# Running sums in the seven-product blocks of a fused three-model kernel, and 16 more blocks in that form

## The chip, the cores and the metric

One core of one Trainium2 chip. The metric is the device time of one execution in microseconds, as the median of three runs: 1971.0 us for the kernel before (1969.97 to 1972.1).

## The reference, cut to what matters

x (1, 256, 1024) in float32 goes through three models one after the other: a first one with two layers (latent attention, then a gated recurrence), here called A and B; a second one of two hybrid layers, L0 and L1; a third one of one layer, C. The change touches L0, L1 and C alone. What is computed of a hybrid layer, around the change:

```python
h = rms_norm(x, norm1_g)
q, k, v, iq, ik, iw, a_in, c_in, g_in = jnp.split(h @ w_in, IN_SPLITS, axis=-1)
y_attn = dsa_attention(q, k, v, iq, ik, iw) @ w_attn_out      # indexer scores, top 64 keys, softmax
a_val, a_gate = jnp.split(a_in, 2, axis=-1)
a = causal_dwconv(a_val * sigmoid(a_gate), conf_conv_w) + conf_conv_b      # 31 taps
y_conf = silu(layer_norm(a)) @ w_conf_out
c_b, c_c, c_x = jnp.split(c_in, 3, axis=-1)
y_sc = (c_b * causal_dwconv(c_c * c_x, sc_conv_w)) @ w_sc_out              # 3 taps
merged = g0 * y_conf + g1 * y_attn + g2 * y_sc                             # g = sigmoid(g_in)
x = x + merged @ w_o
u = causal_dwconv(rms_norm(x, norm2_g) @ w_up, ffn_conv_w) + ffn_conv_b
x = x + (silu(u_gate) * u_val) @ w_down
```

All products are float32. C has retention, block-sparse attention, a gated merge and a feed-forward part of the same sizes.

## The kernel before

Features lie on the partitions, the 256 tokens on the free axis. The weights come in blocks of 128 x 2048 float32 (1 MB) into a ring of two slots, `ring`, by SyncE's queue (L675), in a fixed order (`stream_plan`). SyncE waits for `slot_done` of the slot and, after a seven-product block, for its event `mixed`. Each engine has one queue, written out by hand in its own function, and semaphores between them. One block gives 256 output features for 256 tokens from 1024 input features.

There are two kinds of blocks. A plain one (`halves`) is 16 matmuls of 128x128 weights with 256 columns. A seven-product one (`fast_block`, or `late_block`, where the input comes late) is a Strassen-Winograd form: the block is seen as 2x2 quarters, and seven products of 4 matmuls with 128 columns are made, 28 in all, in place of eight quarter products. A float32 matmul is two instructions in the trace. Its inputs are:
- sums of the input's quarters, made once for a stage by VectorE (`token_sums`, `sum_acts`, L2275 to L2280);
- differences of the weight's quarters, made by GpSimd for each block (`mix`, L1793 to L1805): "mix1" and "mix1b" as one instruction of 1024 columns (L1798), then "mix2" (L1802) and "mixed" (L1805) of 512. For the first block of a stage mix1 and mix1b are two instructions (L1793, L1795). GpSimd waits until the block has landed and the block before in the same buffer is done. It has no other queue for them.

TensorE computes the seven products in the order w0, w3, w2 (slot released here, with `slot_done`), m0, m1, m2, m3, where w are the quarters as they come and m the mixed ones. Each product has its own 128 columns in one of two PSUM banks, "x" and "y". Four main banks make two pairs, taken in turn, so that a block needs the pair of the block two before it. ScalarE copies the first product to `p1c` (`first_product`, L1474). VectorE makes the four output quarters with five adds (`unite`, L2256 to L2265) and frees both banks. VectorE's queue is in the order in which the results are wanted, so an operation in front of a `unite` delays the bank's release.

The stretch that the change rewrites lies in each of L0 and L1 between the gate blocks `g` (12 seven-product blocks) and the attention heads. TensorE's order there: `cx0` (4 seven-product blocks: half of c_c and c_x), among them the small products `spread` and `index_products`; `cx1` (4 plain blocks: the other half); the sums for the layer norm; `cb` (4 plain blocks: c_b); then eight heads, each with one block of `conf` or `sc`. VectorE meanwhile ends the 31-tap convolution (`convolved`, 248 steps of 256 columns with the sum in PSUM), rotates iq, q and k (`rotate_in_place`), adds up the indexer's `scores`, centres the convolution's result (`centred`), does the 3-tap convolution (`short_conv(0)`, `short_conv(1)`: 4 products, 4 first taps, 8 more taps each), finds the top 64 keys (`ranked`, max and match_replace), and makes the mask. ScalarE does the Relu of the indexer (`index_terms`), copies the plain blocks `cx1` out of PSUM, squares for the norm, and issues small transfers from its queue (L1596).

## Time and profile before

| | |
|---|---|
| Median of three runs | 1971.0 us |
| The profiled execution, span from first to last instruction | 1967.1 us |
| The same execution's own time, span and what lies around it | 1971.0 us |
| TensorE busy | 1954.6 us, 99% of the span |
| VectorE busy | 1194.6 us, 61% |
| GpSimd busy | 1119.2 us, 57% |
| ScalarE busy | 402.2 us, 20% |
| Blocks in L0, L1, C that become chained blocks | 195, of them 16 plain before |

Rows of the timeline read: start in us, duration in us, engine, line of the kernel, operation, output tile, input tiles, how many instructions are merged in the row, and in brackets how long the engine was idle before and what ended that. Consecutive instructions of one kind are merged, and a row that begins where another one still runs belongs to a pipelined engine. L712 is the one place from which all matmuls are issued, so a block is told by its operands: `ring` for quarters as they came, `arena` or `h_res` for mixed ones.

### The profile page before, as it was taken

To read this page: it belongs to the slowest core of one execution; us is meant where nothing else is said; L and a number is where in the kernel's file an instruction comes from. 1 tells how busy PE (TensorE), PEld (TensorE's weight loads), DVE (VectorE), ACT (ScalarE), POOL (GpSimd) and SP (SyncE) were. 2 spreads that over 40 slices of the span, in tenths; PEclk is the share of its full clock that TensorE was granted. 3 is DMA by queue.
4 is the path that set the end of the run, shared out by engine and by line. 5 is a ranking of instruction groups with operands and counts; after the bars stand their busy time and mean duration, and the time that the engine had idled before them with its cause. 6 is when DMAs were issued, how large, how long until landed. Compare 5 with 4: busy or idle time off the path is not lost. (4 is left out here: it accounts for less than half of the span.)

```text
span 1967.1 us, 37363 instructions
## 1 busy us (share of the span) xinstructions
PE 1954.6 (99%) x14834; PEld 1848.6 (94%) x14834; DVE 1194.6 (61%) x3033; ACT 402.2 (20%) x978; POOL 1119.2 (57%) x750
## 2 busy tenths in 40 slices
PE   9999999999999999999999999999999999999999
PEld 7788889999899999999999899999999999999998
DVE  4244535989978477524888987667713487554541
ACT  2241521111321222110111222222102025220000
POOL 1000038785176588758678155487776674448783
PEclk9999999999999999999999999999999999999999
DMA  5313445444444454445444343454444442445544
GB/s 212 134 43 132 150 151 179 160 164 139 149 144 143 156 174 167 171 148 172 168 159 168 121 162 131 150 172 172 167 164 161 136 147 97 140 150 172 172 161 140
DMA packets 44267, 299.76 MB, mean 152 GB/s; under 512 B 5440, under 2 KB 6592, under 8 KB 10176
## 3 DMA queue, kind: packets, MB, share of 16 engines
q1 hardware_dynamic: 42560, 295.42, 43.7%
q8 instruction: 119, 1.95, 0.4%
q10 hardware_dynamic: 1536, 1.97, 0.3%
q14 instruction: 52, 0.43, 0.1%
HBM read 294.35 MB, written 1.05 MB: 150 GB/s over the span
## 5 line engine op out<-in xcount | busy, mean ns | idle before, releaser
L712 PE MATMUL bank<-arena,ring 128*128 128x128 f32 (+2 forms) x3854 | 603.4, 310 | 1.2 <-ACT arena L1344 0.6
L712 PEld LDWEIGHTS bank<-arena,ring 128*128 128x128 f32 x3854 | 540.4, 191 | 43.6 <-ACT arena L1344 3.1
L712 PE MATMUL bank<-xn,ring 128*128 128x128 f32 (+3 forms) x3104 | 467.8, 306 | 0.0
L712 PEld LDWEIGHTS bank<-xn,ring 128*128 128x128 f32 (+1 forms) x3104 | 424.4, 191 | 31.1 <-issue 4.4
L712 PE MATMUL bank<-arena 128*128 128x128 f32 (+3 forms) x3048 | 391.5, 284 | 0.0
L712 PEld LDWEIGHTS bank<-arena 128*128 128x128 f32 (+1 forms) x3048 | 364.9, 192 | 9.3 <-issue 1.5
L712 PE MATMUL bank<-arena,h_res 128*128 128x128 f32 x2696 | 322.4, 276 | 2.1 <-POOL h_res L1802 1.2
L712 PEld LDWEIGHTS bank<-arena,h_res 128*128 128x128 f32 x2696 | 310.6, 192 | 5.1 <-POOL h_res L1802 2.4
L1798 POOL TENSOR_TENSOR arena<-ring 128x1024 f32<-128x1024 f32 (+1 forms) x103 | 243.0, 2360 | 124.7 <-DMA ring<-wstream 124.2
L1798 POOL TENSOR_TENSOR h_res<-ring 128x1024 f32<-128x1024 f32 (+1 forms) x95 | 221.7, 2334 | 127.1 <-DMA ring<-wstream 111.9
L1849 DVE SCALAR_TENSOR_TENSOR bank<-arena,par,bank 128x256 f32<-128x256 f32 x640 | 259.5, 483 | 15.3 <-DVE arena L2265 7.7
L1474 ACT ACTIVATE p1c<-bank 128x128 f32<-128x128 f32 x192 | 52.3, 272 | 730.8 <-PE bank L712 730.5
L2259 DVE TENSOR_TENSOR partial<-bank,p1c 128x128 f32<-128x128 f32 x192 | 55.0, 286 | 225.1 <-PE bank L712 224.8
L1805 POOL TENSOR_TENSOR h_res<-ring,h_res 128x512 f32<-128x512 f32 (+1 forms) x111 | 144.3, 1300 | 8.7
L1802 POOL TENSOR_TENSOR h_res<-h_res,ring 128x512 f32<-128x512 f32 (+1 forms) x111 | 143.8, 1296 | 8.7
L1766 POOL TENSOR_TENSOR sq<-sq 128x256 f32<-128x256 f32 (+1 forms) x45 | 34.7, 772 | 187.7 <-ACT sq L1347 169.3
L1793 POOL TENSOR_TENSOR h_res<-ring 128x512 f32<-128x512 f32 x16 | 20.4, 1276 | 211.8 <-DVE arena L2280 83.6
L1802 POOL TENSOR_TENSOR arena<-arena,ring 128x512 f32<-128x512 f32 (+1 forms) x103 | 133.4, 1295 | 8.1
L1805 POOL TENSOR_TENSOR arena<-ring,arena 128x512 f32<-128x512 f32 (+1 forms) x103 | 132.9, 1291 | 8.1
L2256 DVE TENSOR_TENSOR bank<-bank,p1c 128x128 f32<-128x128 f32 x80 | 23.6, 296 | 147.1 <-ACT p1c L1474 145.4
L1313 ACT ACTIVATE arena<-bank 128x256 f32<-128x256 f32 (+6 forms) x104 | 44.0, 424 | 206.1 <-PE bank L712 140.6
L712 PE MATMUL bank<-xn,h_res 128*128 128x128 f32 x648 | 84.9, 276 | 1.1 <-POOL h_res L1805 1.1
(241 smaller groups left out, 1805.0 us busy)
## 6 DMA issues: line engine op xcount, KB each, us to landing
ring<-wstream SPq DMA_DIRECT2D x264, 1024.0 KB, 4.8
ring<-wstream SPq DMA_DIRECT2D x16, 768.0 KB, 4.2
cst<-consts SPq DMA_DIRECT2D x1, 2488.0 KB, 14.7
h_res<-tokens SPq DMA_DIRECT2D x2, 544.0 KB, 5.1
arena<-arena ACTq DMA_DIRECT2D x16, 64.0 KB, 3.4
out<-arena SPq DMA_DIRECT2D x4, 256.0 KB, 5.4
arena<-arena ACTq DMA_DIRECT2D x28, 32.0 KB, 3.1
ring<-wstream SPq DMA_DIRECT2D x2, 288.0 KB, 2.9
```

Of the source, the lines that this page charges most:

```text
L712: return pe.matmul(o, lhs, rhs, start=start, stop=stop, skip_group_check=True)
L1313: ins = act.activation(dst, psum[b][0:rows, 0:T], func, **kw)
L1474: act.activation(p1c[:, b // 2 % 2, :], psum[b][:, 0:P], ACT.Copy).then_inc(*e.step((key, "p1")))
L1766: pool.tensor_tensor(out=acc, in0=acc, in1=squares[:, j, 0:T], op=ALU.add).then_inc(*e.step(event))
L1793: pool.tensor_tensor(out=m[:, 0:size], in0=w[:, size:2 * size], in1=w[:, 0:size], op=ALU.subtract).then_inc(*e.step(("mix1", block)))
L1798: pool.tensor_tensor(out=m[:, 0:2 * size], in0=w[:, size:3 * size], in1=w[:, 0:2 * size], op=ALU.subtract).then_inc(*e.step(("mix1", block)))
L1802: pool.tensor_tensor(out=m[:, 2 * size:3 * size], in0=m[:, size:2 * size], in1=w[:, 0:size], op=ALU.add).then_inc(*e.step(("mix2", block)))
L1805: pool.tensor_tensor(out=m[:, 3 * size:4 * size], in0=w[:, 3 * size:4 * size], in1=m[:, 2 * size:3 * size], op=ALU.subtract).then_inc(*e.s ...
L1849: return dve.scalar_tensor_tensor(out=out, in0=a, scalar=scalar, in1=b, op0=op0, op1=op1)
L2256: dve.tensor_tensor(view[:, 0, 0, :], x[:, 2 * P:3 * P], p1, ALU.add).then_inc(*e.step((key, "c11")))
L2259: dve.tensor_tensor(u2, y[:, 3 * P:4 * P], p1, ALU.add).then_inc(*e.step((key, "u2")))
```

## The change

The seven products of a block (all but those of `down` and the first of `attn`) are now added up in PSUM as running sums, in two banks of 256 used columns. The quarters c11, c12 and c21, c22 lie beside each other. ScalarE copies the running sums out four times per block (`snapshot` 1, 5, 2, 3) into `snaps`, two buffers in turn; TensorE waits for the first three before it goes on adding to the same columns. `unite` is one VectorE add of 512 columns. The slot is released after the sixth product, not after the third. SyncE waits for "spent", the last mix that reads the slot. A stage's first block is mixed in the order mix1, mix2, mixed, mix1b. The plain blocks `cx1` and `cb` become chained blocks too: `cx` has eight, `cb` four, and GpSimd mixes for them. ScalarE's other work is put between the snapshots. VectorE's order in the stretch changes: the convolution takes 12 steps per block (10 before) and ends after the last gate block, centring comes after the second unite of `cx`, the first ranking is split 3, 2, 3. GpSimd's partial sums for the layer norm come two gate blocks earlier, and the gathering of its squares two blocks later.

```diff
+            def chain_block(block, plain, sums, ready=None, token_major=False):
+
+                slot = e.next_block()
+                w = ring[:, slot, :].rearrange("p (s k c) -> p s k c", s=4, c=P)
+                m = mixed_of(block).rearrange("p (s k c) -> p s k c", s=4, c=P)
+
+                def product(place, weight, act, opens=False):
+                    half, col = part_at[place]
+                    for k in range(4):
+                        one, two = (act(k), weight[:, k, :]) if token_major else (weight[:, k, :], act(k))
+                        ins = mm(bank[half], slice(0, P), slice(col, col + P), one, two, opens and k == 0, k == 3)
+                    return ins
+
+                pe.wait_ge(*e.landed(slot))
+                bank, emptied = e.take_pair(block)
+                for when in emptied:
+                    pe.wait_ge(*when)
+                for event in ready or ():
+                    pe.wait_ge(*e.at(event))
+                product("c22", w[:, 0], lambda k: plain(0, k, 0), opens=True).then_inc(*e.done("main_done", ("pe", (block, "p1"))))
+                product("c11", w[:, 3], lambda k: plain(1, k, 0), opens=True)
+                pe.wait_ge(*e.at((sums, "sum", 0)))
+                pe.wait_ge(*e.at(("mix1", block)))
+                product("c12", m[:, 0], lambda k: sums_at_k(sums, 0, k)).then_inc(*e.done("main_done", ("pe", (block, "p5"))))
+                pe.wait_ge(*e.at((block, "s1")))
+                pe.wait_ge(*e.at((sums, "sum", 1)))
+                pe.wait_ge(*e.at(("mix2", block)))
+                product("c22", m[:, 2], lambda k: sums_at_k(sums, 1, k))
+                pe.wait_ge(*e.at(("mixed", block)))
+                product("c21", m[:, 3], lambda k: plain(1, k, 1)).then_inc(*e.done("main_done", ("pe", (block, "p4"))))
+                pe.wait_ge(*e.at((block, "s5")))
+                pe.wait_ge(*e.at((sums, "sum", 3)))
+                product("c12", w[:, 2], lambda k: sums_at_k(sums, 3, k)).then_inc(*e.done(f"slot_done{slot}"))
+                pe.wait_ge(*e.at((block, "s2")))
+                pe.wait_ge(*e.at((sums, "sum", 2)))
+                pe.wait_ge(*e.at(("mix1b", block)))
+                product("c22", m[:, 1], lambda k: sums_at_k(sums, 2, k)).then_inc(*e.done("main_done", ("pe", (block, "t"))))
...
+                def cx(n):
+
+                    chain_block((F, "cx", n // 2, n % 2), of_tokens(xn), (F, "x"))
+
+                cx(0)
                 spread()
-                cx0(F, 1)
-                cx0(F, 2)
+                cx(1)
+                centre_sums(L + "ln", 1, lambda j: sel[:, 0, :], [(L + "ln", "total")])
+                cx(2)
                 pe.wait_ge(*e.at((L + "ikr",)))
                 pe.wait_ge(*e.at((L + "iqr",)))
                 index_products(0, 3)
-                cx0(F, 3)
+                cx(3)
                 index_products(3, 6)
-                halves(L + "cx1", 0, 8, [P, P], x256, S)
+                cx(4)
                 index_products(6, 8)
-                halves(L + "cx1", 1, 8, [P, P], x256, S)
-                centre_sums(L + "ln", 1, lambda j: sel[:, 0, :], [(L + "ln", "total")])
-                halves(L + "cx1", 2, 8, [P, P], x256, S)
-                halves(L + "cx1", 3, 8, [P, P], x256, S)
+                cx(5)
                 b = e.take("beside", (L + "ln", "var"))
                 pe.wait_ge(*e.emptied((L + "ln", "var")))
                 for n, (event, j) in enumerate((((L + "ln", "acc"), 0), ((L + "ln", "sq", 6), 6), ((L + "ln", "sq", 7), 7))):
                     pe.wait_ge(*e.at(event))
                     ins = mm(b, slice(0, P), slice(0, S), C("ones"), sq[:, j, 0:S], n == 0, n == 2)
                 ins.then_inc(*e.side_done((L + "ln", "var")))
+                cx(6)
+                cx(7)
...
+            def snapshot(key, n):
+
+                done, of, to = {1: ("p1", "c22", "c11"), 5: ("p5", "c12", "c22"), 2: ("p4", "c22", "c12"), 3: ("t", "c22", "c21")}[n]
+                (half, col), at = part_at[of], snap_at[to]
+                if n == 1 and snap_before(key):
+                    act.wait_ge(*e.at((snap_before(key), "c22")))
+                act.wait_ge(*e.at(("pe", (key, done))))
+                act.activation(snap(key)[:, at:at + P], psum[e.bank_of((key, half))][:, col:col + P],
+                               ACT.Copy).then_inc(*e.step((key, f"s{n}")))
+
+            def snapshots(key, *meanwhile, early=None):
+
+                snapshot(key, 1)
+                snapshot(key, 5)
+                if early:
+                    early()
+                snapshot(key, 2)
+                for work in meanwhile:
+                    work()
+                snapshot(key, 3)
...
+                snapshots((F, "cx", 0, 0), lambda: gate_tanh_l(11), queries_rms)
+                snapshots((F, "cx", 0, 1))
                 act.wait_ge(*e.at((L + "qkn", 0)))
                 for a, b in ((0, 16), (16, 0)):
                     act.dma_start(qk[a:a + 16, 8:10, :], qk0[b:b + 16, 8:10, :]).then_inc(k_halves, 16)
-                first_product((F, "cx0", 1, 0))
-                index_terms(0, 3)
-                first_product((F, "cx0", 1, 1))
-                index_terms(3, 6)
-                product_in(1, 0)
-                index_terms(6, 8)
-                product_in(1, 1)
-                centred_squares(L + "ln", 8, lambda j: ac[:, j, :])
-                product_in(1, 2)
-                product_in(1, 3)
-                root((L + "ln", "var"), sq[:, 0, 0:S], D, RMS_EPS, (L + "ln", "rms"))
-                act.wait_ge(*e.at((L + "rotated", "q")))
-                for it in range(4):
-                    act.dma_start(qk0[0:32, 2 * it:2 * it + 2, :], qk[32 * it:32 * it + 32, 0:2, :]).then_inc(q_back, 16)
-                for j in range(8):
-                    bias = G(f"{LN_B}.{l}", j)
-                    act.wait_ge(*e.at((L + "zn", j)))
-                    act.activation(yc[:, j, :], ac[:, j, :], ACT.Identity, bias=bias).then_inc(*e.step((L + "z", j)))
-                    act.activation(ac[:, j, :], ac[:, j, :], ACT.Tanh, bias=bias).then_inc(*e.step((L + "zt", j)))
+                snapshots((F, "cx", 1, 0))
+                index_terms(0, 2)
+                snapshots((F, "cx", 1, 1), early=lambda: index_terms(2, 3))
+                index_terms(3, 5)
+                snapshots((F, "cx", 2, 0), rotary_back, lambda: centred_squares(L + "ln", 8, lambda j: ac[:, j, :]), early=lambda: index_terms(5, 6))
+                snapshots((F, "cx", 2, 1), early=lambda: index_terms(6, 8))
+                snapshots((F, "cx", 3, 0), ln_root)
+                snapshots((F, "cx", 3, 1), lambda: norm_gates(0, 2))
+                for q, (first, last) in enumerate(((2, 4), (4, 6), (6, 8), (8, 8))):
+                    snapshots((F, "cb", q, 0), lambda: norm_gates(first, last))
...
+                if block[2:] == (0, 0) and block[1] in ("a", "g", "conf", "o", "up", "mqk", "ret"):
+                    t1, t3, t2, t4 = (m[:, size * c:size * c + size] for c in range(4))
+                    w11, w12, w22, w21 = (w[:, size * c:size * c + size] for c in range(4))
+                    pool.tensor_tensor(out=t1, in0=w12, in1=w11, op=ALU.subtract).then_inc(*e.step(("mix1", block)))
+                    pool.wait_ge(*e.at(("mix1", block)))
+                    pool.tensor_tensor(out=t2, in0=w22, in1=t1, op=ALU.subtract).then_inc(*e.step(("mix2", block)))
+                    pool.wait_ge(*e.at(("mix2", block)))
+                    pool.tensor_tensor(out=t4, in0=w21, in1=t2, op=ALU.subtract).then_inc(*e.step(("mixed", block)))
+                    pool.tensor_tensor(out=t3, in0=w22, in1=w12, op=ALU.subtract).then_inc(*e.step(("mix1b", block)))
+                    e.counts.events["spent", block] = e.counts.events["mix1b", block]
+                    return
...
+            def unite(key, out, cols, *after):
+
                 for event in after:
                     dve.wait_ge(*e.at(event))
+                if len(key) == 4 and chained(key):
+                    dve.wait_ge(*e.at((key, "s3")))
+                    by = "p t (n c) -> p n t c" if key[1] in ("v", "mv", "rv") else "p n (t c) -> p n t c"
+                    x = e.bank_of((key, "x"))
+                    both = banks[:, 512 * x:512 * x + 1024].rearrange("p (t z) -> p t z", t=2)[:, :, 0:2 * P]
+                    dve.tensor_tensor(out[:, :, cols:cols + S].rearrange(by, c=P), both.rearrange("p t (n c) -> p n t c", c=P),
+                                      snap(key).rearrange("p (n t c) -> p n t c", n=2, t=2),
+                                      ALU.add).then_inc(*e.frees((key, "x"), (key, "c11")))
+                    e.counts.events[key, "c12"] = e.counts.events[key, "c22"] = e.counts.events[key, "c11"]
+                    dve.wait_ge(*e.at((key, "c11")))
+                    return
...
-                    convolved(10 * it, 10 * it + 10)
+                    convolved(12 * it, 12 * it + 12)
...
                     unite((F, "g", it, 0), sg[:, 2 * it:2 * it + 2, :], 0)
-                    if it < 11:
-                        convolved(90 + 10 * it, 100 + 10 * it)
-                convolved(200, 214)
-                cx0_in(0)
+                    convolved(108 + 35 * it // 3, 108 + 35 * (it + 1) // 3)
...
+                cx_in(0)
                 spread_norm(L + "qk", range(1), G(g("k_norm_g_2"), 0), qk0[:, 8:10, :], qk0[:, 8:10, :], L + "qkn")
                 query_scales(L + "qk", P ** -0.5)
                 dve.wait_ge(iq_halves, 64 * (l + 1))
                 rotate_in_place(iq0[:, :, :], iq[:, :, :], "idx", slice(0, P), (L + "iqr",))
-                cx0_in(1)
-                convolved(214, 224)
-                cx0_in(2)
-                dve.wait_ge(*e.at((L + "iws",)))
-                scores(0, 3)
-                convolved(224, 232)
-                cx0_in(3)
-                scores(3, 6)
-                convolved(232, 8 * CK)
-                scores(6, 8)
+                cx_in(1)
                 if l == 0:
                     for j in range(ND):
                         dve.wait_ge(*e.at(("N3", "xn", j)))
                 centred(L + "ln", 8, lambda j: ac[:, j, :])
+                cx_in(2)
+                dve.wait_ge(*e.at((L + "iws",)))
+                scores(0, 3)
+                cx_in(3)
+                scores(3, 6)
                 dve.wait_ge(q_rows, 192 * (l + 1))
                 rotate_in_place(qk[:, 0:2, :], qk[:, 2:4, :], "attn", slice(0, P), (L + "rotated", "q"))
+                cx_in(4)
+                scores(6, 8)
                 dve.wait_ge(k_halves, 32 * (l + 1))
                 rotate_in_place(qk0[0:32, 8:10, :], qk[0:32, 8:10, :], "attn", slice(0, 32), (L + "rotated", "k"))
...
+                    pair = slice(2 * q, 2 * q + 2)
+                    unite((F, "cb", q, 0), both_p, 0, *([(L + "ys", 2 * q - 1)] if q else [(L + "ac", 6), (L + "ac", 7)]))
                     for t in range(2):
-                        j, key = 2 * q + t, (L + "cb", q, t)
-                        dve.wait_ge(*e.at(("pe", key)))
-                        dve.wait_ge(*e.at((L + "sct", j, 2)))
-                        dve.tensor_tensor(ys[:, j, :], psum[e.bank_of(key)][:, 0:S], ys[:, j, :],
-                                          ALU.mult).then_inc(*e.frees(key, (L + "ys", j)))
+                        dve.wait_ge(*e.at((L + "sct", 2 * q + t, 2)))
+                    dve.tensor_tensor(ys[:, pair, :], both_p, ys[:, pair, :], ALU.mult).then_inc(*e.step((L + "ys", 2 * q + 1)))
...
                 short_conv(0)
-                ranked(0, TOPK // 16)
+                cx_in(5)
+                ranked(0, 3)
                 dve.wait_ge(*e.at((L + "ln", "rms")))
                 dve.reciprocal(sq[:, 0, 0:S], sq[:, 0, 0:S]).then_inc(*e.step((L + "ln", "inv")))
                 dve.wait_ge(*e.at((L + "ln", "inv")))
+                cx_in(6)
                 for j in range(ND):
                     stt(ac[:, j, :], ac[:, j, :], G(g(LN_G), j), sq[:, 0, 0:S], ALU.mult, ALU.mult).then_inc(*e.step((L + "zn", j)))
+                cx_in(7)
+                short_conv(1)
                 branch_b(0)
-                short_conv(1)
+                ranked(3, 5)
                 branch_b(1)
                 for j in range(ND):
                     dve.wait_ge(*e.at((L + "zt", j)))
@@ -2482,7 +2615,7 @@
                 for j in range(ND):
                     dve.wait_ge(*e.at((L + "yc", j)))
                 token_sums((F, "yc"), yc)
-                ranked(TOPK // 16, TOPK // 8)
+                ranked(5, TOPK // 8)
                 branch_b(2)
```

## Rows read from the trace of the kernel before

**Rows 1.** The page: busy time of each engine, and granted clock in 40 slices.
```profile
PE 1954.6 (99%) x14834; PEld 1848.6 (94%) x14834; DVE 1194.6 (61%) x3033; ACT 402.2 (20%) x978; POOL 1119.2 (57%) x750
...
PEclk9999999999999999999999999999999999999999
```
**Rows 2.** TensorE's waits, the largest: line, releaser, total us, times, longest us.
```profile
PE bank L711 <- DVE arena L2146: 2.1, 3, 0.8
```
**Rows 3.** Timeline of TensorE in C.up: w2 ends where these rows start.
```profile
1799.73 2.84 PE L712 MATMUL bank<-arena 128*128 128x128 f32 x24
...
1805.99 2.84 PE L712 MATMUL bank<-arena,h_res 128*128 128x128 f32 x24
```
**Rows 4.** Timeline of TensorE in L0: stretch's start, plain cb, first head.
```profile
455.88 1.95 PE L712 MATMUL bank<-xn,ring 128*128 128x128 f32 x16
...
516.74 27.79 PE L712 MATMUL bank<-xn,ring 128*128 128x256 f32 x128
544.37 0.82 PE L712 MATMUL bank<-arena 128*128 128x128 f32 x4
...
552.13 0.55 PE L711 MATMUL bank<-cst,arena 128*128 128x128 f32 x3 [0.69 <-DVE arena L2146]
```
**Rows 5.** Timeline in C.up: one block's adds on VectorE, ScalarE's copy.
```profile
1803.83 0.42 DVE L2261 TENSOR_TENSOR partial<-bank,partial 128x256 f32<-128x256 f32 x1
...
1805.12 0.69 DVE L2753 TENSOR_TENSOR arena<-arena,bank 128x512 f32<-128x512 f32 x1 [0.20 <-DVE bank L2265]
...
1806.19 0.28 ACT L1474 ACTIVATE p1c<-bank 128x128 f32<-128x128 f32 x1 [5.98 <-PE bank L712]
```
**Rows 6.** Timeline of GpSimd in L0.up and C.up; the first row is TensorE's.
```profile
703.73 2.84 PE L712 MATMUL bank<-arena,h_res 128*128 128x128 f32 x24
...
710.21 2.36 POOL L1798 TENSOR_TENSOR h_res<-ring 128x1024 f32<-128x1024 f32 x1 [2.52 <-DMA ring<-wstream]
...
1798.45 2.36 POOL L1798 TENSOR_TENSOR h_res<-ring 128x1024 f32<-128x1024 f32 x1 [1.10 <-DMA ring<-wstream]
...
1802.23 1.26 POOL L1805 TENSOR_TENSOR h_res<-ring,h_res 128x512 f32<-128x512 f32 x1
1804.93 2.35 POOL L1798 TENSOR_TENSOR arena<-ring 128x1024 f32<-128x1024 f32 x1 [1.44 <-DMA ring<-wstream]
...
1807.36 1.60 POOL L1802 TENSOR_TENSOR arena<-arena,ring 128x512 f32<-128x512 f32 x1
```
**Rows 7.** Timeline of L0's stretch: GpSimd, VectorE alone, ScalarE's transfers.
```profile
475.60 1.27 POOL L1805 TENSOR_TENSOR arena<-ring,arena 128x512 f32<-128x512 f32 x1
...
514.13 3.24 DVE L1849 SCALAR_TENSOR_TENSOR arena<-arena,par 128x256 f32<-128x256 f32 x8
...
516.95 2.44 ACTq L1596 DMA_DIRECT2D arena<-arena  x4
...
542.55 1.27 POOL L1793 TENSOR_TENSOR h_res<-ring 128x512 f32<-128x512 f32 x1 [34.06 <-issue]
```
**Rows 8.** Busy time in windows of L0's stretch: PE, PEld, DVE, ACT, POOL.
```profile
455.90:500.00 44.10, 44.10 (x321) 40.88 (x320) 40.34 (x95) 8.15 (x18) 17.93 (x12) 1.00 0.37 127
...
516.70:544.40 27.70, 27.70 (x130) 24.37 (x130) 27.46 (x92) 8.37 (x18) 1.85 (x2) 1.00 0.48 162
```
**Rows 9.** VectorE's adds in SBUF while GpSimd works: L0's heads, attn, C.up.
```profile
608.34 2.35 POOL L1798 TENSOR_TENSOR arena<-ring 128x1024 f32<-128x1024 f32 x1 [2.83 <-DMA ring<-wstream]
609.46 1.37 DVE L2275 TENSOR_TENSOR arena<-arena 128x128 f32<-128x128 f32 x1 [1.57 <-ACT arena L1313]
...
610.87 1.31 DVE L2277 TENSOR_TENSOR arena<-arena 128x128 f32<-128x128 f32 x1
...
627.54 1.37 DVE L2275 TENSOR_TENSOR arena<-arena 128x256 f32<-128x256 f32 x1
...
1805.85 1.98 DVE L2275 TENSOR_TENSOR arena<-arena 128x512 f32<-128x512 f32 x1
```
**Rows 10.** Timeline of TensorE: the first matmuls of the program.
```profile
1.11 6.05 PE L712 MATMUL bank<-sq 128*128 128x256 f32 x16 [1.11 <-POOL small L1750]
```

284 lines of the change are left out of this document (155 added, 129 removed).

## Prediction

> **What bounds the kernel now.** I read the page first: TensorE is busy for 1954.6 of the 1967.1 us of the profiled span, VectorE for 1194.6, GpSimd for 1119.2 [rows 1]. The list of TensorE's waits, read next, adds up to some 9 us in 11 pairs; the largest is 2.1 us in three waits of up to 0.8 us [rows 2]. So the time is the sum of TensorE's blocks. A change gains only if it shortens that sum, and loses whatever it makes TensorE wait. The timeline of C.up gives the price of a seven-product block: the third product ends at 1799.73 in one block and at 1805.99 in the next, so 6.26 us for 56 recorded instructions [rows 3]. The four plain blocks L0.cb run from 516.74 to 544.37, 6.91 us each [rows 4].
>
> **The gain.** 16 plain blocks become seven-product blocks: 16 x (6.91 - 6.26) = 10.4 us off TensorE. The other blocks keep their 28 products, so nothing is gained there on TensorE. VectorE's five adds per block (of 0.28 to 0.42 us, 1.7 us in all) become one add of 512 elements, like the 0.69 us ones beside them [rows 5]. That is about 1.0 us less VectorE work per block, off the path. ScalarE copies four times instead of once, 0.28 us each, starting 0.2 us behind TensorE [rows 5]. A snapshot that TensorE waits for is thus there 0.2 + 0.28 + about 0.1 = 0.6 us after its product. TensorE does 8 of its 28 matmuls (1.8 us) in between for the first two snapshots and 4 of them (0.9 us) for the third. It is free as long as ScalarE does nothing else at that moment.
>
> **The slack that the new order uses up.** The ring slot is released after 12 of 28 matmuls before, after 24 of 28 now: 12/28 x 6.26 = 2.7 us later. GpSimd starts the next subtraction 5.20 us behind the release (release 1799.73, start 1804.93) and has all three done 5.04 us after its start (1798.45 to 1803.49) [rows 3, 6]. So the last mix is there 5.4 + 5.2 + 5.0 - 12.5 = 3.1 us after the start of the block that needs it; it was needed at 5.4 us, and is now needed at 3.6 us. A slack of 4.9 us becomes 0.4 to 0.5 us, in all 195 changed blocks. What eats it: (a) late landings. GpSimd starts at 710.21 for a slot released at 703.73, 6.5 us [rows 6]; seven such blocks (5.99 to 7.65 us) lie in stages without other cover, and what they have over the slack adds to 5 us. (b) VectorE's sums over SBUF in the up stages lengthen a mix from 1.27 to 1.60 us [rows 6]; two groups of four per up stage, 0.5 us each, three stages: 3 us. (c) The second block of six stages, whose mix starts late because the first one's is on the path: 0.5 us each, 3 us. Sum 11 us; bounds 3 (most of it covered) and 20 (each twice as often).
>
> **The stretch that decides.** GpSimd does nothing for the plain blocks: it ends its mixes at 476.87 and starts the next at 542.55, after 34 us in which it had nothing to do [rows 7]. In that gap VectorE is fully busy: 40.34 of 44.10 us in its first part, 27.46 of 27.70 us in its last [rows 8]. Rows from L0's head stage show what happens when both are busy: VectorE's 128x128 add takes 0.28 us alone, and 1.37, 1.31, 1.31 us while GpSimd subtracts; each one ends 0.1 us after a GpSimd instruction ends, one per GpSimd instruction [rows 9]. I see this for all operations with two SBUF inputs and for tensor_scalar between SBUF tiles, and for none that reads PSUM (the 0.69 us ones of rows 5 ran under a subtraction), nor for max, match_replace and reciprocal. By the Trainium skill (SBUF — State Buffer, "Who interferes with whom") a VectorE instruction with two SBUF inputs contends with a GpSimd one that reads SBUF, and the pair is locked for a whole instruction; by that rule, which speaks against this change, the trace agrees.
>
> The new blocks bring 3 subtractions each, 5.0 us, so GpSimd works 5.0 of every 6.3 us through the stretch. VectorE's operations there that need the shared reads are some 90 a layer: rotations of iq, q, k (9), 8 to centre, 16 scores, two short convolutions of 16 (3.24 us for eight of one's, alone [rows 7], 5.6 us with the cheaper eight), 8 + 8 of the norm and its gate, 4 sums, 4 of the mask: about 38 us alone. The others (12 unites, ranking, products from PSUM, the end of the convolution) are about 33 us.
>
> Walked through L0, with time 0 at the end of the last gate block (455.88) [rows 4]; landings by 5.1 us, one such operation per mix while GpSimd has work, free running when it has none:
> - cx block 3 starts at 13.8. The three rotations of iq alternate with its mixes: last mix at 18.8, needed at 17.6, and the one before just late. TensorE waits 1.6 us.
> - cx block 4 starts at 22.9. Its third snapshot stands on ScalarE behind a Relu that waits for the first score, which stands on VectorE behind eight centring subtractions (four of them alternate with mixes) and a unite: score at 30.1, snapshot 30.8, needed 28.3. Waits 2.6 us.
> - cx block 6 starts at 41.8. Its first snapshot stands behind rotary_back (VectorE's rotation done at 42.6, then four DMA issues, 2.44 us for four [rows 7]), eight squares (2.8 us) and the fourth snapshot of block 5: done at 48.5, needed at 44.5. Waits 4.0 us.
> - cx block 8 wants its pair of banks at 59.8. VectorE's unite that frees it stands behind four scores, three rotations and the first short convolution: 23 operations, ten of them held by a mix, done at 72.0. Waits 12.3 us.
> - cb block 3 wants its banks at 90.9. The unite before stands behind the ranking, eight norm products and the second short convolution (three mixes each for two blocks and more): 102.0. Waits 11.2 us.
> - first head: gates, sums, ranking, mask; logits masked at 121.2, ScalarE's snapshot behind the exponentials: 3.1 us against the 0.7 us wait that is there now [rows 4].
> Sum 34.8 - 0.7 = 34.1 us a layer, 68.2 us for both layers, which have the same order. Bounds: VectorE and GpSimd must at least share time. From 9.2 us on GpSimd has 61 us of work, VectorE 38 us of its held kind, less about 0.2 us saved at each of some 40 alternations: they end at 9.2 + 61 + 38 - 8 = 100 us, and the head's chain (7 us) follows: 107 against 96.2 - 5.3 = 91 us for TensorE alone, so 16 us a layer is the least, if nothing else ever waits and all is contended. If GpSimd's work for the first head falls outside, 11 us. The upper end is 45 us, if the waits shift each other.
>
> **Sum.** Profiled execution: 1967.1 us of span and 3.9 us around it, 1971.0, which is also the median. 1971.0 - 10.4 + 11 + 68.2 + 5 = 2044.8 us.
>
> **Rivals.**
> - The engines fit each other: VectorE's port work falls into GpSimd's pauses, because it has 26 us less to do a layer before the stretch and its convolution ends 34 us earlier (495.8 now, 5.9 us after the gate blocks then). Then the floor above holds, 11 to 16 us a layer: 1971.0 - 10.4 + 3 to 11 + 2 x (11 to 16) = 1985 to 2003. For it: each TensorE wait leaves GpSimd idle. Against it: the order of the two queues is fixed.
> - The other side, faster: the alternation doesn't hold for these operations (rows 9 show 128-column adds; a 0.33 us operation of 256 columns or a score may slip in two at a time). It decides from the point where more than two pass per mix: then VectorE's 71 us lie under TensorE's 83, only the ScalarE wait of block 6 stays (about 2 us a layer), and 1971.0 - 10.4 + 4 + 0 to 6 gives 1965 to 1971, of which the lower half is the likelier. Against it: an add of 256 columns takes 1.37 us at 627.54, and the one of 512 columns at 1805.85 takes 1.98 us [rows 9]; the trace has 11 such rows of 256 and 26 of 512 columns over 1.1 us.
> - The snapshots break TensorE's stream by themselves: a wait in front of a matmul costs 0.19 us of reload even if it comes in time by a hair. Three of them in 195 blocks, one in five costing this, is 22 us more, 2067. Against it: mixes were waited for in every block before, and TensorE's 6.26 us show nothing of it.
> - The change isn't what it says: a snapshot order that serializes blocks would show as 0.6 us in every block, 117 us, over 2150. Little speaks for it: the cover is 0.9 us.
>
> **How the numbers follow.** Forecast with its parts (2015 to 2070): 0.58. Engines fit (1985 to 2015): 0.17. Not held: faster by over 0.2% (under 1967) 0.12, within 0.2% 0.05. Snapshots break the stream or waits shift each other (over 2070): 0.08. A measurement of this kernel can tell 0.2%, 4 us, from no change. The range 1988 to 2075 leaves out the two on the fast side and the far end. Slower is 0.58 + 0.17 + 0.08 = 0.83.
>
> **What would show it.** Right: two waits of about 10 us a layer on TensorE ended by VectorE's unite, in the stretch of cx and cb; VectorE's short convolution at 10 us and more for 16 operations; GpSimd's mixes at 1.4 us in place of 1.27; waits of 0.2 to 1 us for mixes in the up stages. Wrong: a stretch from last gate block to first head under 92 us; more than one held operation per mix; or TensorE blocks over 6.4 us throughout.

## The result

The changed kernel takes 2048.8 us (median of four runs, 2046.7 to 2053.0) against 1970.5 us (1969.9 to 1972.1) of the kernel before, measured beside it: 1.040 times as long, 95% interval 1.0386 to 1.0416. The profiled execution has a span of 2047.3 us, 80.2 more than before; the medians differ by 78.3. In the runs of this case an execution is 1.8 to 2.1 us longer than its span. So the 1967.1 us of before fit an execution of some 1969 us better than the one of 1971.0 that the table ahead gives, and the two differences agree.

The page of the kernel after: busy time with instruction counts, and the granted clock by slices (the two rows of [rows 1]).

```profile
PE 1971.6 (96%) x15218; PEld 1868.4 (91%) x15218; DVE 1098.8 (54%) x2325; ACT 552.6 (27%) x1563; POOL 1211.1 (59%) x798
...
PEclk9999999999899999999999899999999999999999
```

TensorE should have been busy for 10.4 us less than before; it is busy for 17.0 more. So 27.4 us went into matmuls at half clock and into starts after waits; two slices of the granted clock show an 8. Its waits, longest totals first: line, releaser, total us, times, longest (rows 2 had 2.1 us as its largest):

```profile
PE banks L743 <- DVE arena L2380: 20.5, 2, 10.3
PE banks L743 <- ACT snaps L1556: 12.1, 12, 1.9
PE banks L743 <- DVE banks L2380: 11.1, 4, 4.8
PE banks L743 <- ACT arena L1412: 8.8, 10, 2.4
...
PE banks L743 <- POOL h_res L1921: 3.4, 4, 0.9
```

L2380 is `unite`, L1556 a snapshot, L1412 ScalarE's scaling of the residual in front of the up stages. Where the time went by place is read from the start of one and the same matmul in both timelines. Those of after:

```profile
378.81 1.04 PE L743 MATMUL banks<-sq,cst 128*16 128x256 f32 x4
...
580.74 0.55 PE L742 MATMUL banks<-cst,arena 128*128 128x128 f32 x3 [0.34 <-DVE arena L2270]
...
700.22 1.46 PE L743 MATMUL banks<-sq,cst 128*128 128x256 f32 x6
...
1219.16 0.55 PE L742 MATMUL banks<-cst,arena 128*128 128x128 f32 x3 [0.34 <-DVE arena L2270]
...
1834.03 1.46 PE L743 MATMUL banks<-sq,cst 128*128 128x256 f32 x6
```

In before they start at 374.60, 552.13 [rows 4], 665.68, 1156.62 and 1755.49. With the markers between them, the lag grows as follows:

| from, to | L0 | L1 | C |
|---|---|---|---|
| gate and q stages | 4.2 | 3.9 | 0.7 |
| gate blocks | 0.2 | in the next | |
| last gate block to first head | 24.2 | 22.8 | |
| heads to the end of the last o block's sums | 5.9 | 3.2 | 4.8 (heads), 6.2 (to the sums) |
| up, down | 1.3 | 1.1 | 1.7 |

So 47 us lie in the two stretches and 33.2 us elsewhere, where 11 were forecast. The stretch of L0, TensorE's rows with a wait or at half clock (the first four belong to cx blocks 3, 4, 4 and 6):

```profile
477.67 1.13 PE L743 MATMUL banks<-arena,h_res 128*128 128x128 f32 x8 [0.70 <-POOL h_res L1925]
...
490.54 4.45 PE L743 MATMUL banks<-arena 128*128 128x128 f32 x20 [1.75 <-ACT snaps L1556]
494.92 3.78 PE L743 MATMUL banks<-xn,ring 128*128 128x128 f32 x16
...
509.27 1.16 PE L743 MATMUL banks<-arena 128*128 128x128 f32 x8 [1.13 <-ACT snaps L1556]
...
530.90 3.75 PE L743 MATMUL banks<-xn,ring 128*128 128x128 f32 x16 [10.24 <-DVE arena L2380]
534.44 2.93 PE L743 MATMUL banks<-arena 128*128 128x128 f32 x16
...
557.30 3.11 PE L743 MATMUL banks<-xn,ring 128*128 128x128 f32 x13 [4.75 <-DVE banks L2380]
```

This is what VectorE and GpSimd did before the wait of 10.24 us ended: the first short convolution (L2560, L2563, L1973: 16 operations), then the unite, beside GpSimd's subtractions. The eight operations of L1973 are shown as seven and one.

```profile
520.37 2.48 DVE L2560 TENSOR_TENSOR arena<-arena 128x256 f32<-128x256 f32 x4
522.77 2.13 DVE L2563 TENSOR_SCALAR arena<-arena,par 128x256 f32<-128x256 f32 x4
524.83 2.84 DVE L1973 SCALAR_TENSOR_TENSOR arena<-arena,par 128x256 f32<-128x256 f32 x7
527.60 2.55 DVE L1973 SCALAR_TENSOR_TENSOR arena<-arena,par 128x256 f32<-128x256 f32 x1
530.08 0.67 DVE L2380 TENSOR_TENSOR arena<-banks,snaps 128x512 f32<-128x512 f32 x1
...
522.65 2.11 POOL L1928 TENSOR_TENSOR arena<-ring,arena 128x512 f32<-128x512 f32 x1
524.72 5.16 POOL L1921 TENSOR_TENSOR h_res<-ring 128x1024 f32<-128x1024 f32 x1
```

The 16 operations take 9.8 us. Seven of them ran at their usual pace inside one GpSimd instruction, which took 5.16 us and not 2.36 [rows 6]; the eighth took 2.55 us and ended 0.27 us behind that instruction. So GpSimd was held first, by seven operations, and then held the eighth. Each GpSimd instruction here does hold one VectorE operation, as forecast, but others pass before it: either engine may be the one that is held, and the pair takes about what both would take one after the other (3.24 + 2.36 against 5.3). When the turn changes hands isn't shown by any run. The Trainium skill says this too (SBUF — State Buffer, "Who interferes with whom"): the order of issue decides who blocks. The prediction had used only its other sentence.

The next reading is the q stages. Of their growth 3.5 us in each layer (1.8 and 1.7) lie at two places: the v block and the first iq block. L0's v block, kernel after:

```profile
352.60 1.95 PE L743 MATMUL banks<-ring,xn 128*128 128x128 f32 x16
352.91 2.35 POOL L1921 TENSOR_TENSOR h_res<-ring 128x1024 f32<-128x1024 f32 x1 [3.15 <-PE banks L743]
355.40 1.13 PE L743 MATMUL banks<-h_res,arena 128*128 128x128 f32 x8 [0.85 <-POOL h_res L1921]
```

The block in front has its mixed weights in the same buffer, `h_res`. So GpSimd waits for TensorE to end that block, not for a landing. In before it waited there too:

```profile
352.19 2.36 POOL L1798 TENSOR_TENSOR h_res<-ring 128x1024 f32<-128x1024 f32 x1 [5.33 <-PE bank L712]
```

But TensorE then had 12 matmuls with plain weights before it wanted the first mix (2.7 us); now it has 8 (1.8 us), and that mix takes 2.35. These are the four waits for "POOL h_res L1921" in the list above.

The last reading is the boundary before the up stage. ScalarE in L0, kernel after:

```profile
689.60 0.28 ACT L1556 ACTIVATE snaps<-banks 128x128 f32<-128x128 f32 x1 [1.51 <-PE banks L743]
689.89 1.28 ACT L1406 ACT_TABLE_LOAD   x1
...
691.30 0.89 ACT L1412 ACTIVATE arena<-x_res,par 128x256 f32<-128x256 f32 x2
...
691.93 1.10 PE L743 MATMUL banks<-arena,ring 128*128 128x256 f32 x4 [2.37 <-ACT arena L1412]
```

In before ScalarE had its only copy of the last o block behind it at 656.5 and did the table load and the first scalings while TensorE still multiplied (until 659.6):

```profile
656.49 1.28 ACT L1338 ACT_TABLE_LOAD   x1
```

Now they stand behind that block's fourth snapshot. No step of the prediction looked at this place.

### The profile page after: what moved, and what is told of

Read it like the earlier page. It is cut to its first block, busy times and chain, and to the rows that moved or that the text cites. A ratio compares the mean times of both kernels' runs of the same rounds, so it can differ in the third digit from the quotient of the medians.

```text
span 2047.3 us, 38407 instructions
## 1 busy us (share of the span) xinstructions
PE 1971.6 (96%) x15218; PEld 1868.4 (91%) x15218; DVE 1098.8 (54%) x2325; ACT 552.6 (27%) x1563; POOL 1211.1 (59%) x798
## 4 chain that ended last, share of the span: by engine, by line
PE 79%; DVE 10%; POOL 4%; ACT 3%; DMA 2%; issue 2%; ACTq 0%; DVEq 0%; SPq 0%; POOLq 0%
PE banks L743 79%; DMA ring<-wstream 2%; DVE tmp L1973 1%; DVE arena L1973 1%; DVE arena L2336 1%; DVE arena L2563 1%; POOL arena L1921 1%; PE banks L742 1%; POOL h_res L1921 1%; DVE xn L1994 0%; DVE arena L2327 0%; POOL arena L1928 0%; POOL arena L1925 0%; POOL h_res L1911 0%; POOL h_res L1909 0%
## 5 line engine op out<-in xcount | busy, mean ns | idle before, releaser
L743 PE MATMUL banks<-arena,ring 128*128 128x128 f32 (+2 forms) x3982 | 629.0, 310 | 11.9 <-ACT arena L1412 8.8
L743 PEld LDWEIGHTS banks<-arena,ring 128*128 128x128 f32 x3982 | 560.0, 192 | 57.4 <-issue 10.7
L1556 ACT ACTIVATE snaps<-banks 128x128 f32<-128x128 f32 x780 | 213.7, 277 | 984.3 <-PE banks L743 981.4
L743 PE MATMUL banks<-arena 128*128 128x128 f32 (+4 forms) x3240 | 437.1, 286 | 9.4 <-ACT snaps L1556 8.3
L743 PE MATMUL banks<-xn,ring 128*128 128x128 f32 (+3 forms) x2848 | 395.5, 294 | 30.0 <-DVE arena L2380 20.5
L743 PEld LDWEIGHTS banks<-arena 128*128 128x128 f32 (+1 forms) x3240 | 399.0, 193 | 21.7 <-ACT snaps L1556 9.8
L743 PEld LDWEIGHTS banks<-xn,ring 128*128 128x128 f32 (+1 forms) x2848 | 365.4, 195 | 49.1 <-issue 35.3
L743 PE MATMUL banks<-arena,h_res 128*128 128x128 f32 x2888 | 360.1, 276 | 13.7 <-POOL h_res L1907 4.9
L1921 POOL TENSOR_TENSOR arena<-ring 128x1024 f32<-128x1024 f32 (+1 forms) x111 | 263.4, 2373 | 159.0 <-DMA ring<-wstream 158.7
L743 PEld LDWEIGHTS banks<-arena,h_res 128*128 128x128 f32 x2888 | 340.2, 192 | 17.5 <-issue 7.2
L1921 POOL TENSOR_TENSOR h_res<-ring 128x1024 f32<-128x1024 f32 (+1 forms) x103 | 247.8, 2405 | 142.0 <-DMA ring<-wstream 125.5
L1973 DVE SCALAR_TENSOR_TENSOR banks<-arena,par,banks 128x256 f32<-128x256 f32 x640 | 259.0, 484 | 2.7
L2380 DVE TENSOR_TENSOR arena<-banks,snaps 128x512 f32<-128x512 f32 x120 | 82.8, 690 | 248.6 <-ACT snaps L1556 248.2
L2380 DVE TENSOR_TENSOR banks<-banks,snaps 128x512 f32<-128x512 f32 x75 | 52.3, 698 | 161.7 <-ACT snaps L1556 161.7
L1973 DVE SCALAR_TENSOR_TENSOR arena<-arena,banks 128x512 f32<-128x512 f32 (+2 forms) x71 | 42.1, 596 | 98.0 <-ACT arena L1836 41.2
```

The source lines that it names most:

```text
L743: return pe.matmul(o, lhs, rhs, start=start, stop=stop, skip_group_check=True)
L1556: act.activation(snap(key)[:, at:at + P], psum[e.bank_of((key, half))][:, col:col + P], ACT.Copy).then_inc(*e.step((key, f"s{n}")))
L1921: pool.tensor_tensor(out=m[:, 0:2 * size], in0=w[:, size:3 * size], in1=w[:, 0:2 * size], op=ALU.subtract).then_inc(*e.step(("mix1", block)))
L1973: return dve.scalar_tensor_tensor(out=out, in0=a, scalar=scalar, in1=b, op0=op0, op1=op1)
L2380: dve.tensor_tensor(out[:, :, cols:cols + S].rearrange(by, c=P), both.rearrange("p t (n c) -> p n t c", c=P), snap(key).rearrange("p (n t ...
```

## The experiments

All ran beside the kernel before, whose medians were 1969.8 to 1970.9 us.

| kernel | median us | ratio, 95% interval |
|---|---|---|
| after | 2048.8 | 1.0386 to 1.0416 |
| plain_stretch | 2010.9 | 1.0191 to 1.0225 |
| boundary | 2039.5 | 1.0335 to 1.0369 |
| small_mixes | 2001.4 | 1.0140 to 1.0181 |
| reordered | 2055.3 | 1.0422 to 1.0486 |
| splitmix | 2042.7 | 1.0339 to 1.0381 |
| scalar_order | 2039.5 | 1.0333 to 1.0369 |
| sixteen_alone | 2025.2 | 1.0258 to 1.0292 |
| sixteen_small | 1984.0 | 1.0056 to 1.0090 |
| plain_repaired | 1997.8 | 1.0126 to 1.0160 |
| dummy | 1994.7 | 1.0108 to 1.0142 |
| dummy_half | 1985.9 | 1.0066 to 1.0099 |
| waits | 1999.4 (one run) | |

### Is it GpSimd's subtractions? small_mixes

```diff
+                elif block[1] in ("cx", "cb"):
+                    pool.tensor_tensor(out=m[:, 0:8], in0=w[:, size:size + 8], in1=w[:, 0:8], op=ALU.subtract)
...
+                    pool.tensor_tensor(out=m[:, 3 * size:3 * size + 8], in0=w[:, 3 * size:3 * size + 8], ...)
```

> The changed kernel, with GpSimd's three subtractions of each cx and cb block done on 8 columns instead of 1024, 512 and 512: the weights' sums of these blocks are left out but for 8 columns. The waits and the order stay. Port theory (VectorE's operations with two SBUF inputs and GpSimd's exclude each other for a whole instruction): the 16 operations of a short convolution take 5.4 us and not 9.7 to 13.6, the waits in front of cx block 8 and cb block 3 (10.2 and 4.8 us a layer) are gone, a stretch takes 92 to 95 us and not 120, and the time is 1993 to 2000 us. Rival (the order of VectorE's and ScalarE's queues alone, without any contention): the unites stand as far back, both waits stay at half or more, and the time is 2030 us or more.

Measured: 2001.4 us, 47.4 less. VectorE's timeline at the same place:

```profile
508.02 1.41 DVE L2572 TENSOR_TENSOR arena<-arena 128x256 f32<-128x256 f32 x4
509.36 1.12 DVE L2575 TENSOR_SCALAR arena<-arena,par 128x256 f32<-128x256 f32 x4
510.41 3.24 DVE L1985 SCALAR_TENSOR_TENSOR arena<-arena,par 128x256 f32<-128x256 f32 x8
```

5.6 us instead of 9.8, and the waits of 10.2 and 4.8 us are gone. So the loss in the stretch comes from GpSimd's subtractions: the same order and waits with almost no GpSimd work in them lose nothing there. The edit takes away a little more than the change brought, for four of its 12 blocks a layer had subtractions before; `dummy`, below, only adds some. But the stretch gains nearly nothing either: first head minus last gate block is 0.4 us shorter than in before, where 8 converted blocks should have saved 5.2 us a layer. Waits for snapshots and for banks (1.13, 0.29, 0.78, 0.82, 0.65 and 0.35 us) take most of it.

### The price of a subtraction: dummy, dummy_half

```diff
...
+                        for _ in range(16):
+                            pool.tensor_tensor(out=m[:, 1024:1536], in0=m[:, 0:512], in1=m[:, 512:1024],
+                                               op=ALU.subtract).then_inc(*e.step((L + ".dummy",)))
+                            pool.wait_ge(*e.last())
```

> The kernel before, with 16 GpSimd subtractions (128x512, SBUF to SBUF, into a part that nobody reads) put into GpSimd's idle gap of 34 us in both layers; nobody waits for them. Port theory: they hold about 16 of VectorE's operations for a whole instruction each, some 16 x (1.4 - 0.35) = 17 us more for VectorE, which was fully busy in the stretch and was waited for 0.7 us at the first head; so GpSimd's 16 take 25 us or more instead of 21, and TensorE waits 8 to 17 us a layer for VectorE: 1987 to 2005 us. Rival (GpSimd's work beside VectorE costs nothing as such; what costs in the changed kernel is that its blocks wait for unites and snapshots): 1970 to 1973 us.

> The kernel of dummy (1994.7 us, 16 idle GpSimd subtractions a layer in the kernel before), with 8 a layer. Theory: VectorE already sets the end of this stretch, so each subtraction costs from the first on, 23.8/32 = 0.74 us: 1970.5 + 12 = 1982.4 us (1980 to 1985). Rival: VectorE has some room there (reads from PSUM, ranking, its waits) that takes in the first ones; then under 1977 us.

Measured: 23.8 us for 32 subtractions that nobody waits for, 15.1 us for 16. The first price is 0.94 us each, that of the second half 0.54. The port theory holds (its rival said 0 to 2 us). The straight line, 12 us for the 16, was too low: the 95% interval of the 15.1 us is 13 to 20. Perhaps the later ones meet VectorE's ranking, which reads one input; that wasn't tried. The prices hold what TensorE then lost in clock: in dummy it ran for 8.9 us at half clock behind its two longest waits, which is 4.5 of the 23.8 us. In dummy TensorE waits for the third plain cb block's bank behind VectorE:

```profile
538.62 1.62 PE L712 MATMUL bank<-xn,ring 128*128 128x256 f32 x3 [7.85 <-DVE arena L2455]
```

In units of 512 columns the 12 blocks of small_mixes have 48 a layer: 47.4/96 = 0.49 us each, near the second price.

### Shorter instructions: splitmix

```diff
+                    for c in range(4):
+                        at = part * c
+                        pool.tensor_tensor(out=m[:, at:at + part], in0=w[:, size + at:size + at + part], in1=w[:, at:at + part], ...)
```

> The changed kernel, with GpSimd's three subtractions of each cx and cb block (1024, 512 and 512 columns) cut into eight of 256 columns; the same sums. Theory (an exclusive read is held for a whole instruction, and each alternation lets one VectorE operation through): shorter instructions let a VectorE operation through after 0.7 us instead of 1.3 to 2.5, so the short convolutions take 7 to 9 us instead of 9.7 and 13.6, the waits in front of cx block 8 and cb block 3 shrink by half, and the time falls by 10 to 25 us to 2024 to 2039. Rival (both share the port by columns, or not at all): GpSimd pays only the overhead of more instructions, and the time is 2047 to 2060 us.

Measured: 6.1 us less, between the ranges of the theory and of its rival. VectorE is let through sooner (L0's first short convolution takes 7.1 us), but the mixes come later: waits for GpSimd of up to 3.9 us appear. If what is shared is the sum of both engines' work, cutting it finer moves little; that fits, and is not shown.

### Is it the order? reordered, scalar_order

```diff
                 cx_in(4)
                 scores(6, 8)
+                cx_in(5)
                 rotate_in_place(qk0[0:32, 8:10, :], ...)
-                short_conv(0)
-                cx_in(5)
-                ranked(0, 3)
...
                 cx_in(7)
+                short_conv(0)
+                branch_b(0)
+                ranked(0, 3)
+                branch_b(1)
                 short_conv(1)
-                branch_b(0)
                 ranked(3, 5)
-                branch_b(1)
```

> The changed kernel, with VectorE's order in the stretch changed alone: the unites of cx blocks 6, 7 and 8 and of cb 1 and 2 each stand at the place where TensorE's block ends, and the first short convolution behind them instead of ahead of the unite of block 6. Theory of the prediction: the long waits come from unites behind 16 held operations, so the waits of 10.2 and 4.8 us and the half-clock matmuls behind them (2.7 and 1.0 us) go; but the held work itself stays, and the least for it was 16 us a layer over 91 us, so a stretch takes 107 to 112 us instead of 120: 2048.8 - 2 x (8 to 13) = 2023 to 2033 us. Rival 1: all of it comes back in front of the first head, 2045 to 2052 us. Rival 2: the order was the whole cause, a stretch takes 93 to 97 us, about 1997 us.

Measured: 2055.3 us, 6.5 more; rival 1, and a little beyond it. The wait in front of cx block 8 is gone, and TensorE waits at cb block 3 and in front of the first head's block instead:

```profile
546.72 3.76 PE L743 MATMUL banks<-xn,ring 128*128 128x128 f32 x16 [7.31 <-DVE banks L2380]
...
573.69 3.50 PE L743 MATMUL banks<-arena,ring 128*128 128x128 f32 x16 [9.59 <-DVE banks L2380]
```

The second of them is partly the fault of this order, which has the unite of cb block 3 behind four sums and a ranking; a better one may gain a few microseconds and wasn't tried. By this reading it can't gain much: in the kernel after VectorE is busy, held time included, for 63.4 of the 67.3 us that end at the first head's mask.

```profile
509.90:577.20 67.30, 51.49 (x413) 50.64 (x412) 63.38 (x126) 15.88 (x47) 43.43 (x25) 0.87 0.32 110
```

```diff
-                snapshots((F, "cx", 1, 1), early=lambda: index_terms(2, 3))
+                snapshots((F, "cx", 1, 1), lambda: index_terms(2, 3))
```

(with the edit of boundary below, and C's squares of the group norm behind the next head's first two snapshots)

> The changed kernel, with three pieces of ScalarE's queue moved: the boundary's first six tiles ahead of the last o block's fourth snapshot (measured alone: 9.3 us less), the third Relu of the index scores from ahead of the third snapshot of cx block 4 to behind it, and C's squares of the group norm from ahead of the next head's first two snapshots to behind them. Theory: a snapshot behind another piece of ScalarE's work that waits for VectorE is a cost of its own. The Relu's wait of 1.75 us and the half-clock matmuls behind it (4.1 us) go in both layers, 8 to 11 us, and in C's heads 3 to 4.8 us: 2048.8 - 9.3 - 9.5 - 4 = 2026 us (2021 to 2031). Rival: in the stretch VectorE's queue sets the end, so what TensorE doesn't wait at cx block 4 it waits at cx block 8; then only the boundary and C's heads count, and it is 2034 to 2037 us.

Measured: 2039.5 us, no less than boundary alone; the rival's reason, and 2.5 us over its range. The waits of L0's stretch show the exchange: the 1.75 us and the half clock behind it are gone, cx block 6 waits 4.38 us instead of 1.13, and what is left at cx block 8 is 6.72. (In boundary alone cx blocks 4, 6 and 8 of L0 wait 1.73, 2.88 and 5.53, 10.1 us against 11.1 here.)

```profile
507.43 1.25 PE L743 MATMUL banks<-arena 128*128 128x128 f32 x8 [4.38 <-ACT snaps L1559]
...
527.17 3.75 PE L743 MATMUL banks<-xn,ring 128*128 128x128 f32 x16 [6.72 <-DVE arena L2388]
```

C's heads didn't change (snapshots waited for 1.40, 1.07 and 1.37 us, and 1.15, 1.02 and 1.37 in after). There the third snapshot stands behind a table load of 1.28 us and the softmax, as ScalarE's rows of the kernel after show; that this is the cause is read, not tested.

```profile
1716.32 1.28 ACT L1517 ACT_TABLE_LOAD   x1
1718.43 0.49 ACT L1517 ACTIVATE arena<-arena,small,q_scale 128x128 f32<-128x128 f32 x1 [0.83 <-DVE small L2259]
...
1719.50 0.26 ACT L1556 ACTIVATE snaps<-banks 128x128 f32<-128x128 f32 x1
```

### The two halves of the change: plain_stretch, sixteen_alone, sixteen_small

```diff
-        fast(n + "cx", "w_in_2", l, 4, 2, ...)
-        fast(n + "cb", "w_in_2", l, 4, 1, ...)
+        fast(n + "cx0", "w_in_2", l, 2, 2, ...)
+        pl(n + "cx1", "w_in_2", l, 2, 2, 8, two(co + 1536, co + 2560))
+        pl(n + "cb", "w_in_2", l, 2, 2, 8, seq(co))
```

> The changed kernel, with the 16 blocks of cx's second half and cb put back as plain blocks and VectorE's order there put back with them; the running sums stay everywhere else. Theory: the trace after puts 24.2 and 22.8 us of the loss between the last gate block and the first head of the two layers, and 33.2 us elsewhere, and the two parts don't depend on each other. So this kernel takes 1970.5 + 33 = 2003 us (1998 to 2008). Rival: what is lost elsewhere is knock-on from the stretch (its transfers, its VectorE queue); then most of the 33 us go as well, and it takes 1975 to 1990 us. By the sum in the prediction, 11 us elsewhere, it would be 1982 us.

Measured: 2010.9 us, 3 us over the range of the theory. Running sums alone cost 41 us. Outside the stretches the loss is about that of after (35 and 33 us of span); 4.4 and 4.1 us more lie in the two stretches, where the expectation had nothing (a wait of 0.96 us for a mix, and 2.59 us for a snapshot at the first head).

```diff
         def chained(block):
-            return block[1] != "down" and block[1:] != ("attn", 0, 0)
+            return block[1] in ("cx", "cb")
```

(all others in the form of before)

> The 16 converted blocks and the four of cx's first half alone have running sums, with the changed kernel's order; all other blocks have the form of the kernel before (five adds, ring slot released after 12 of 28 products, one snapshot). Theory: small_mixes showed that GpSimd's subtractions in the stretch cost 47 us by themselves, and nothing outside the stretch is lost with the form of before: 1970.5 + 43 to 50 = 2014 to 2021 us. Rival 1: with five adds in each block before the stretch VectorE comes into it later, and the stretch costs more, 2025 to 2045 us. Rival 2: the stretch costs as much only because the ring's slack was lost before it; then 1985 to 2005 us.

> The kernel of sixteen_alone (2025.2 us), with GpSimd's subtractions of the cx and cb blocks on 8 columns, as in small_mixes: the sums of weights of these blocks are left out but for 8 columns. Theory: the reads that GpSimd and VectorE can't do together are the whole loss of the 16 blocks, and nothing is lost outside; then it takes 1970.5 less the 10.4 us that TensorE saves, plus what small_mixes still waited for snapshots and the banks in the two stretches, 4.8 us each, and 3.9 us in front of the first cx block of each layer, where VectorE's convolution is late: 1960 to 1978 us, the likelier part under 1970.5. Rival: the snapshots and the single large add cost more than the seven products save even without GpSimd; then 1980 us or more.

Measured: 2025.2 and 1984.0 us. The 16 blocks alone cost 54.9 us, of which the subtractions are 41.2 (with those of cx's first half, as in small_mixes). The first is at the lower end of its rival 1. The second is 4 us inside its rival's range, but not for its rival's reason: of the 13 us that stay, 11 lie ahead of the stretches: with five adds in each gate block, the changed kernel's denser convolution is late, and the first cx block waits for its bank and then runs at half clock.

```profile
455.68 1.06 PE L743 MATMUL banks<-xn,arena 128*128 128x128 f32 x8
460.59 3.45 PE L743 MATMUL banks<-xn,ring 128*128 128x128 f32 x16 [3.85 <-DVE arena L2459]
```

That is a fault of this combination, not of the 16 blocks. Behind it the stretch is 0.3 us shorter than in before, much as in small_mixes. The halves cost 41 and 55 us, 96 together, and the whole change 78. The 18 us between are about what each half pays at places where the whole change doesn't: 8.5 us in the stretches of plain_stretch and 11 us in front of those here.

### Outside the stretch: boundary, plain_repaired

```diff
                 for it in range(3):
-                    snapshots((F, "o", it, 0))
-                boundary(..., xg_f)
+                    snapshots((F, "o", it, 0), *([lambda: to_n2(range(3))] if it == 2 else []))
+                to_n2(range(3, 4))
```

> The changed kernel, with ScalarE's table load and its scaling and squares of the first six residual tiles put ahead of the fourth snapshot of the last o block, where they stood in effect before; three places (both layers and C). Theory: TensorE's 2.4 us wait at each first up block, with 0.2 us behind it and the matmuls at half clock after it, comes from that order alone; 4 to 4.7 us go at each place, so the time falls by 12 to 14 us to 2035 to 2037. Rival: the wait is the tail behind the last snapshot (unite 0.70, residual 0.69, scaling 0.5), which is as long with either order; then it falls by under 4 us in all.

Measured: 9.3 us less, short of the theory and far over its rival. The 2.37 us waits fall to 0.6. By the markers the places themselves give back 3.1, 2.0 and 2.9 us; the rest is a cheaper stretch of L0 (20.9 us against 24.2, though the edit comes only behind it) less 2.4 us more in L0's up stage. So a few microseconds of these totals seem to differ between executions of the same code.

> The kernel of plain_stretch (2010.9 us: running sums, no converted blocks), with the boundary and C's group-norm squares moved in ScalarE's queue as in scalar_order, and with q, k, v and iq of both layers in the form of the kernel before. Theory: of the 41 us that the running sums cost, the boundary is 9, C's heads 3 to 4.8, and the slack of the ring in the q stages, lost where the slot is released after 24 of 28 products, 8: 2010.9 - 9 - 4 - 8 = 1990 us (1986 to 1995). Rival: the late landings of the q stages don't depend on the form of the block; then 1997 to 2002 us.

Measured: 1997.8 us, 13.1 less than plain_stretch. The q stages gave what the theory said: the sums behind them start 0.5 us later than in before and not 4.1, and in L1 the lag grows by 0.4 and not by 4.5.

```profile
375.07 1.04 PE L744 MATMUL banks<-sq,cst 128*16 128x256 f32 x4
```

The edit puts the whole form of before back there, so it doesn't tell the later release of the slot from the earlier need of the first mix; the rows of the v block speak for the latter. C's heads did nothing, as above. By the markers of the two profiled executions the boundaries gave 8 us and the q stages 7.7, but these two differ by 15.2 us where the medians differ by 13.1. So the total came out at the number of the rival, for another reason. Every version is slower than the kernel before.

### The clock: waits

```diff
+                    if q in (0, 2):
+                        pe.wait_ge(*e.at((L + "probe", q)))
                     halves(L + "cb", q, 8, [P, P], x256, S)
```

> The kernel before, with four waits of TensorE put in: ahead of the first and the third block of cb it waits for 1 and 2 GpSimd subtractions (128x512) in L0 and for 4 and 8 in L1, each 1.3 us alone, which GpSimd starts when TensorE's block before has ended. Theory (a), that a wait of over 10 us may cost the clock and a short one doesn't: the matmuls behind the 1 and 2 subtractions run at full clock, those behind 8 at half of it, 16 matmuls in 3.5 us instead of 1.8. Theory (b), from the trace after, where matmuls ran at half clock behind waits of 1.75, 2.4, 4.8 and 10.2 us: each of the four waits but perhaps the shortest is followed by 1 to 4 us of lost time, with no order by the length of the wait. Total by (b): 1.5 + 2.8 + 5.3 + 10.5 us of waits, up to 1.3 us for each by contention, and 4 to 12 us of clock, 1995 to 2005 us.

TensorE's rows behind the four waits:

```profile
518.58 1.78 PE L712 MATMUL bank<-xn,ring 128*128 128x256 f32 x7 [1.65 <-POOL h_res L1845]
...
535.85 4.63 PE L712 MATMUL bank<-xn,ring 128*128 128x256 f32 x10 [3.19 <-POOL h_res L1845]
...
1135.35 4.85 PE L712 MATMUL bank<-xn,ring 128*128 128x256 f32 x13 [5.65 <-POOL h_res L1845]
...
1162.49 15.94 PE L712 MATMUL bank<-xn,ring 128*128 128x256 f32 x64 [11.28 <-POOL h_res L1845]
```

The one execution took 1999.4 us. Two blocks take 13.82 us undisturbed. Behind the waits of 1.65, 3.19, 5.65 and 11.28 us the next two took 14.1, 16.8, 15.9 and 15.8: 0.3, 2.9, 2.0 and 2.0 us lost. Theory (b). In the first microseconds behind the second wait the granted clock is 0.50 of full, 1.2 GHz:

```profile
518.60:525.00 6.40, 6.40 (x30) 5.65 (x31) 6.37 (x23) 0.67 (x2) 0.00 (x0) 1.00 0.34 123
535.90:540.00 4.10, 4.10 (x10) 3.29 (x11) 3.90 (x10) 0.00 (x0) 0.00 (x0) 0.50 0.29 118
```

But a wait of a given length doesn't always cost the clock. In dummy_half TensorE waits 3.81 us in L0 and 3.78 us in L1 at the same place. Behind the first the granted clock is full, behind the second half:

```profile
534.70:538.00 3.30, 3.30 (x16) 2.91 (x17) 3.30 (x12) 3.30 (x9) 0.00 (x0) 1.00 0.13 50
1147.30:1150.60 3.30, 3.30 (x9) 2.66 (x8) 3.30 (x12) 3.30 (x10) 0.00 (x0) 0.50 0.01 2
```

And a short wait can cost as much as a long one. Behind the wait of 1.75 us in after, the next 36 matmuls, some of them of 256 columns, took 7.95 us (490.54 to 498.49). The same 36 took 4.81 us in small_mixes, where TensorE didn't wait in front of them (487.36 to 492.17), so 3.1 us were lost:

```profile
487.36 2.99 PE L743 MATMUL banks<-arena 128*128 128x128 f32 x20
490.28 2.05 PE L743 MATMUL banks<-xn,ring 128*128 128x128 f32 x16
```

Counted in the same way, 2.7 us were lost behind the wait of 10.24 us.

## Why the prediction came out

The forecast was 2044.8 us, and 2048.8 was measured. The main mechanism was right, but that the number is so near is luck. By the spans the waits of the two stretches were forecast 27.7 us too high, the clock 11.9 and the rest of the kernel 22.2 us too low.

- **The gain**: the price of a block was right, 6.25 us (539.89 to 546.14 in cb). The working forgot that waits of under a microsecond come with it; with next to no subtractions the 16 blocks give 0.9 us in both layers together, not 10.4.
- **Waits in the stretch**: 34.1 us a layer forecast, 20.0 in L0 and 20.5 in L1 found. By place, forecast and L0: cx block 3 1.6 and 1.0, block 4 2.6 and 1.75, block 6 4.0 and 1.1, block 8 12.3 and 10.2, cb block 3 11.2 and 4.8, first head 2.4 and 1.1. Every place was right, and every releaser but one: 0.8 us at the first head were ended by VectorE's unite. The mis-sized term is one VectorE operation per subtraction: up to seven passed while GpSimd was held. The rival "not held" took this as its condition (more than two pass per mix) and concluded that the loss would go. The condition came true and the conclusion didn't, because the time that VectorE doesn't wait GpSimd waits.
- **The clock**: 5 us forecast for four waits. The stretches are 24.2 and 22.8 us longer; with 5.2 saved and 20.0 and 20.5 waited, 9.4 and 7.5 us are left for slow matmuls and starts, 16.9 in all. The step that failed took the price to belong to waits of over 10 us. The one of 1.75 us lost 3.1 us, the one of 10.24 us 2.7. By the Trainium skill (TensorE: Matmul & The Clock Gate, "The HAM clock gate") the array drops to 1.2 GHz when it has idled; in the trace of after this is so behind eight of its nine longest waits in and behind the stretches, 1.75 to 10.25 us. The exception is the 2.37 us wait in front of L1's up stage (24 matmuls behind it at full clock). The prediction's upper end, 2.6 us each, was nearer than the 1.3 that its sum took; what the sum lacked above all is the short waits.
- **Elsewhere**: 11 forecast, 33.2 found. (a) Late landings, 5 forecast: TensorE waits seven times, 0.12 to 0.45 us and 1.35 in all, for a mix that stands behind a late landing; the lag grows by some 3 us at these places. The growth of 4.2 and 3.9 us in the q stages is for the most part something else (3.5 us a layer). The slack was worked out for the last mix and for a GpSimd that starts when the slot has landed; where two blocks in succession share a buffer, it starts when TensorE is done, and the first mix is the one that comes late. (b) and (c), 6 forecast, are 4.1 us in the up stages. Missed are the boundary (8.0 us by the places that the experiment mended) and C's heads (4.8). Both break one sentence of the prediction: a snapshot "is free as long as ScalarE does nothing else at that moment". It was not followed through the places where ScalarE does something else, and its reverse, that ScalarE's other work now stands behind four snapshots, was not seen at all. Of the other 8 us, most of them between the heads and the sums behind o, some 2 are such late mixes; the rest was not taken apart.
- **The slack** of 0.4 us on the last mix held: in C.up it is just used up, and where VectorE's sums lengthen a subtraction to 1.60 us, TensorE starts that product 0.4 us late (1892.84 against 1892.45).
- **Rivals**: "engines fit" and "not held" gave 1985 to 2003 and 1965 to 1971 us, and small_mixes and dummy show why they fell. "Snapshots break the stream" and "the change isn't what it says" fell with the undisturbed blocks of 6.25 us.

## What to carry to other kernels

Before giving an idle engine work, ask which other engine is full at that time and what the two share; here GpSimd's idle 34 us were VectorE's full ones, and each added subtraction cost 0.5 to 0.9 us. Before taking plain work from the front of a block, ask what the first differing piece waits for, a landing or a buffer. When the full engine sets the end, moving a wait by reordering only chooses where it is paid. And when one copy becomes four, walk through every piece of work on that engine that now stands behind the last of them.

## What the runs showed of the hardware

- When VectorE (two SBUF inputs) and GpSimd meet, either may be held: seven 256-column operations of 0.47 us passed while one GpSimd instruction stood, which took 5.16 us instead of 2.36, and the eighth was then held for 2.55 us.
- The price of a wait in clock doesn't grow with the wait: 0.3, 2.9, 2.0 and 2.0 us behind 1.65, 3.19, 5.65 and 11.28 us. A short wait may cost nearly twice its own length (3.1 us behind 1.75), and a longer one nothing (full clock behind 3.81 us in dummy_half).
